# Hybrid scan, retention and latent-attention diffusion step: prologue, early mixer and the stage between scan and attention reordered

## The chip, the cores and the metric

One core of a Trainium2 chip runs the whole program. Time is device microseconds (us) of that core. Engines: TensorE (PE, its weight loads PEld), VectorE (DVE), ScalarE (ACT), GpSimd (POOL), and SyncE (SP), which here only issues DMAs. Every engine works through a list of its own, in order, and waits on semaphores.

## The reference, cut to what matters

128 context tokens and 256 latent tokens (T = 384 columns) run through two layers of width 1024, all in float32:

```python
h = rmsnorm(x) * (1 + scale1) + shift1
u = h @ w_in                      # split among three head groups
y_ssd = rmsnorm((scan_f + scan_b + d_skip * xs) * silu(z)) # xs: conv of width 5, silu
y_ret = silu(g) * groupnorm(retention_f + retention_b)
q = rmsnorm(u_q) @ w_uq           # rank 256, 4 heads, 64 + 32 rotary
k, v = rmsnorm(u_kv) @ w_ukv      # rank 128, cached context keys before
y_mla = softmax(q k / sqrt(96)) v
x = x + gate1 * (concat(y_ssd, y_ret, y_mla) @ w_out)
h = rmsnorm(x) * (1 + scale2) + shift2
x = x + gate2 * swiglu(h)
```

Scales, shifts and gates come from `silu(cond) @ w_ada + b_ada`, 1024 x 6144 a layer.

## The kernel before, in words

Channels lie on the 128 partitions, tokens on the free axis. A float32 product against a big weight is made of three matmuls in a reduced format: weights and activations are each split in a high part (`whi`, `h_hi`) and a rest (`wlo`, `h_lo`); ACT rounds the high part (`split_hi`, L966) and DVE subtracts for the rest (`split_lo`, L1278). Weights come in blocks of 1 MB over two slots of `stage`; SP issues each load when the slot's split is done. `w_in` is 11 blocks of 256 columns (`win_block`), `w_out` 4, the feed-forward 22 and 16. A w_in block leaves PSUM by `win_out` on ACT; in layer 1 DVE first scales it by the norm (`evac`) and ACT adds a shift (`add_shift`). The modulation matmuls (`ada_block`) are strewn between as filler for PE.

**Prologue (layer 0).** SP loads the early constants, the first half of x, weight block 0, the dt weights, block 1, then, after two of ACT's loads have landed, the small weights and the other constants. ACT issues the second half of x and eight chunks of 1 MB of modulation weights (`ada0`, L1014). ACT makes Silu of the condition (for which a table is loaded), loads the table of Exp and Ln again, and squares the second half of x (L1021); DVE squares the first half (L1368) and adds the pairs (L1372); PE sums over partitions (L540). The norm factor is made by `rstd`: ACT's Ln and Exp give a start value, DVE's four steps (L1306 to L1310) refine it. For each of eight chunks PE multiplies (`ada0_chunk`), DVE copies the rows out (`ada0_taken`, L1377), PE sums them (`ada0_sum`, L562), DVE makes scale and shift and h (`modulated`, `normed`, `normed_low`), and PE runs its tiles of dt and block 0 (`dt_tile`, `win_tile`). On DVE the split of block 0 stands after `modulated(0)`.

**Early mixer (both layers).** Blocks 0, 1 and 2 fill the padded `upad`, on which DVE runs a convolution of five taps for three pairs of channel tiles (`conv_pair`, 8 instructions, L1441); ACT makes the first tap (`first_taps`) and the Silu (`silu_channels`, L1037). Step sizes (`step_sizes`) give the decays, whose running sums PE makes (L617 to L629), ACT copies (`cum`, `tedt`, `cd`, `cumt`) and DVE splits (L1499 to L1505). PE then transposes the convolved values of the three chunks (`turn_values`, L640), runs block 4, transposes the keys (L652), and makes the chunk states (L662) from products that POOL computes (L1785) once all copies of the transpositions are there. On DVE the order in layer 1 is: block 0 out, split 2, block 1 out, dt bias, split 3, step sizes, pair 0, block 2 out, the cumulative rows, pair 1 (`conv_pair(2)`), split 4, pair 2, block 3 out. On PE the transposition of the third chunk, which needs block 3 out of PSUM, stands before block 4.

**Scan.** Six steps (chunk, group) follow, each beside one of the blocks 5 to 10.

**Between scan and attention.** PE (L718 to L824): four retention states, two modulation blocks, then for each of three chunks the retention scores, a sum of squares (gated scan output, query latent, key latent, one after the other in PSUM bank 7, `mean_square`), a modulation block, and the retention values; the key rotation; the group mean of the retention output (`mu_ps`), queries (L792) with the group's sum of squares between head 2 and 3, query rotations (L800), keys (L809), values (L817). DVE runs four `rstd` here, three of width T and one of width 2T, and the elementwise work behind each; the buffer `gsq` holds all squares, `rt` the rotated part. Everything must be done, the last `rstd` too, before attention's first score (L847).

## Time and profile before

| | |
|---|---|
| median of 3 runs | 1102.44 us (1101.33 to 1104.98) |
| the profiled execution, its own time | 1104.6 us |
| its span, first to last instruction | 1102.7 us |
| mean granted clock of PE | 0.979 |
| PE busy | 1034.7 us (94%) |
| DVE, ACT, POOL busy | 632.0, 440.1, 98.3 us |
| moved by DMA | 159.56 MB, mean 145 GB/s |

A granted clock of 1.00 is 2.4 GHz, 0.50 is 1.2 GHz. A row of the timeline reads: start, busy us, engine, line, operation, output <- inputs, shape, count, and in brackets the idle time of the engine before it with what ended it. Idle time counts only where it lies on the chain that ends last; a busy time next to idle time of PE says who was waited for. A float32 matmul stands as two records. `q` after an engine marks the DMAs that it issues.

### The profile page before, as it was taken

The numbers are of one execution on the slowest core, as the hardware profiler recorded it, in microseconds if no ns is written. First come the engines' busy times: TensorE is split into PE (matmuls) and PEld (weight loads), VectorE is DVE, ScalarE is ACT, GpSimd is POOL, SyncE is SP. The second block draws the span as 40 slices with busy tenths as digits, with TensorE's granted clock in tenths as the row PEclk, the third lists the DMA queues.
The fourth block names the chain that finished last, engine by engine and source line by source line (L and its number), as shares of the span: only waits on it lengthen the run. The fifth ranks groups of instructions, "written<-read, shape, count | busy, mean of one in ns | idle before, by whom it ended". The sixth has DMA issues, their size and how long they took to land.

```text
span 1102.7 us, 16365 instructions
## 1 busy us (share of the span) xinstructions
PE 1034.7 (94%) x6520; PEld 942.9 (86%) x6520; DVE 632.0 (57%) x1138; ACT 440.1 (40%) x682; POOL 98.3 (9%) x99
## 2 busy tenths in 40 slices
PE   3999997899999999999999599889999999999996
PEld 2697994589999989999999589647899999999995
DVE  5567767657655544434356677685675545544333
ACT  3155446336433332333335444642563334333231
POOL 0003323003000000001000042400010000000010
PEclk9899999899999999999999899998999999999998
DMA  9642345313333468333353222550233333543431
GB/s 386 258 188 86 115 153 190 124 39 122 118 140 123 170 250 313 132 121 129 116 222 153 77 87 79 217 209 1 77 115 114 123 143 115 184 174 105 131 131 57
DMA packets 30679, 159.56 MB, mean 145 GB/s; under 512 B 3425, under 2 KB 4385, under 8 KB 19873
## 3 DMA queue, kind: packets, MB, share of 16 engines
q1 hardware_dynamic: 29328, 149.63, 37.4%
q10 hardware_dynamic: 1296, 9.18, 2.0%
q8 instruction: 38, 0.62, 0.2%
q14 instruction: 17, 0.13, 0.0%
HBM read 156.27 MB, written 2.52 MB: 144 GB/s over the span
## 4 chain that ended last, share of the span: by engine, by line
PE 86%; DVE 8%; ACT 3%; issue 1%; DMA 1%; POOL 0%; DVEq 0%; SPq 0%; ACTq 0%; POOLq 0%
PE ps L464 25%; PE ps L466 24%; PE ps L465 24%; PE ps L491 2%; DVE v L1441 2%; PE ps L865 1%; DVE wlo L1278 1%; PE ps L847 1%; PE ps L792 1%; ACT whi L966 1%; DMA x<-x_dram 1%; PE ps L662 1%; PE ps L856 1%; PE ps L684 1%; PE ps L710 1%
## 5 line engine op out<-in xcount | busy, mean ns | idle before, releaser
L464 PE MATMUL ps<-h_hi,whi 128*128 128x386 f32 (+1 forms) x1120 | 387.7, 346 | 0.2
L466 PE MATMUL ps<-h_hi,wlo 128*128 128x386 f32 (+1 forms) x1120 | 382.4, 341 | 0.0
L465 PE MATMUL ps<-h_lo,whi 128*128 128x386 f32 (+1 forms) x1120 | 381.5, 341 | 0.0
L1278 DVE TENSOR_TENSOR wlo<-stage,whi 128x2048 fp32r<-128x2048 f32 (+1 forms) x106 | 223.4, 2108 | 151.9 <-ACT whi L966 151.9
L966 ACT ACTIVATE whi<-stage 128x2048 fp32r<-128x2048 f32 (+1 forms) x106 | 185.9, 1753 | 228.1 <-PE ps L466 203.9
L464 PEld LDWEIGHTS ps<-h_hi,whi 128*128 128x128 f32 x1120 | 213.5, 191 | 11.1 <-issue 9.7
L465 PEld LDWEIGHTS ps<-h_lo,whi 128*128 128x128 f32 x1120 | 213.9, 191 | 0.3
L466 PEld LDWEIGHTS ps<-h_hi,wlo 128*128 128x128 f32 x1120 | 212.8, 190 | 0.1
L464 PE MATMUL ps<-hid_hi,whi 128*128 128x384 f32 x352 | 118.3, 336 | 0.0
L466 PE MATMUL ps<-hid_hi,wlo 128*128 128x384 f32 x352 | 118.3, 336 | 0.0
L465 PE MATMUL ps<-hid_lo,whi 128*128 128x384 f32 x352 | 118.3, 336 | 0.0
L1326 DVE COPY shifted<-ps 128x4 f32<-128x4 f32 x55 | 8.8, 161 | 109.0 <-PE ps L466 108.6
L466 PEld LDWEIGHTS ps<-hid_hi,wlo 128*128 128x128 f32 x352 | 66.2, 188 | 0.0
L464 PEld LDWEIGHTS ps<-hid_hi,whi 128*128 128x128 f32 x352 | 66.2, 188 | 0.0
L465 PEld LDWEIGHTS ps<-hid_lo,whi 128*128 128x128 f32 x352 | 66.2, 188 | 0.0
L1337 DVE SCALAR_TENSOR_TENSOR x<-ps,modl,x 128x128 f32<-128x128 f32 x96 | 35.4, 410 | 11.6 <-PE ps L466 11.6
L1837 POOL TENSOR_TENSOR ny<-nv 128x384 f32<-128x384 f32 x2 | 2.2, 1093 | 441.5 <-ACT nv L1244 441.5
L491 PE MATMUL ps<-adas,cond 128*32 128x256 f32 x640 | 39.9, 383 | 0.0
L1200 ACT ACTIVATE adas<-ps,att 128x384 f32<-128x384 f32 (+1 forms) x24 | 12.2, 510 | 55.6 <-DVE att L1684 55.6
L491 PEld LDWEIGHTS ps<-adas,cond 128*32 128x32 f32 x640 | 18.1, 109 | 18.2 <-issue 8.7
L1002 ACT ACTIVATE hid_hi<-nt 128x384 f32 (+1 forms) x22 | 11.6, 525 | 51.8 <-DVE nt L1726 51.8
L1002 ACT ACTIVATE hid_hi<-ny 128x384 f32 (+1 forms) x22 | 11.6, 525 | 51.7 <-DVE ny L1726 51.7
(269 smaller groups left out, 1147.2 us busy)
## 6 DMA issues: line engine op xcount, KB each, us to landing
stage<-wf_dram SPq DMA_DIRECT2D x44, 1024.0 KB, 4.8
adas<-wada_dram SPq DMA_DIRECT2D x80, 512.0 KB, 5.6
stage<-win_dram SPq DMA_DIRECT2D x22, 1024.0 KB, 4.8
stage<-wf_dram SPq DMA_DIRECT2D x32, 704.0 KB, 4.1
stage<-wout_dram SPq DMA_DIRECT2D x8, 1024.0 KB, 5.4
adaf<-wada_dram ACTq DMA_DIRECT2D x6, 1024.0 KB, 17.6
small<-small_dram SPq DMA_DIRECT2D x2, 1202.5 KB, 9.0
adas<-wada_dram ACTq DMA_DIRECT2D x2, 1024.0 KB, 29.9
```

The lines of the kernel that those rows point to most:

```text
L464: mm(out, ah, bh, start=(k == 0), stop=False)
L465: mm(out, ah, bl, start=False, stop=False)
L466: return mm(out, al, bh, start=False, stop=(k == n - 1))
L491: last = mm(ps[j * CW:(j + 1) * CW, 4, half * 256:half * 256 + 256], cond[:, k, :], adas[:, b % 4, j * 256:(j + 1) * 256], start=(b == 0), ...
L662: last = mm(ps[d * 64:d * 64 + 64, 6 - s // 2 * 2, g * 256:g * 256 + 256], bt[:, c, g * 64:g * 64 + 64], vte[s][:, g * 256:g * 256 + 256], ...
L684: last = mm(ps[:, 5 + d, hh * P:hh * P + P], sel[:, h:h + 1].to_broadcast([P, P]), cumt[:, i0:i0 + P], start=True, stop=True)
L966: f(whi[:, g % 2, 0:width], stage[:, g % 2, 0:width], ACT.Copy).then_inc(w_hi, 1)
L1002: f(hid_hi[:, bass.ds(i * 2 + j, 1), :], (ny, nt)[j][:, 1:2, :], ACT.Copy).then_inc(hid_hi_ready, 1)
L1200: f(pr[:, i % 2, 0:nk * P], ps[:, i % 2, 0:nk * P], ACT.Exp, bias=att[:, 1, i:i + 1], scale=SCALE, accum_out=att[:, 2, i:i + 1]).then_inc( ...
L1278: tt(wlo[:, g % 2, 0:width], stage[:, g % 2, 0:width], whi[:, g % 2, 0:width].bitcast(F32), ALU.subtract)\
L1337: last = stt(xm, ps[:, bank:bank + 1, t0:t1], gm, xm, ALU.mult, ALU.add)
L1441: ins = stt(v[:, a, :], upad[:, a, w:w + CONVT], sc(C_CW + w * 6 + a), v[:, a, :], ALU.mult, ALU.add)
```

## The change

No arithmetic is added or left out except that two of the norms share one `rstd`, so that a layer has five. What is moved:

- Prologue: the first half of x is loaded by ACT's queue, ahead of the second; SP holds weight block 1 back until chunk 1 of `ada0` has landed. ACT squares its half of x before the Silu of the condition (the table of Exp and Ln is loaded ahead of it, Silu's and again Exp's behind it), and splits block 0 before `rstd`. DVE splits block 0 first of all; the row copy of chunk 1 comes after `modulated(0)`.
- Early mixer: on DVE pair 0 comes before block 1 in layer 1, pair 1 right after the step sizes in both layers. On ACT the cumulative rows come before `win_out(2)` and its split; the first taps of pair 2 come after the first four Silus; the copy of the third transposition comes after the stacked copies. On PE `turn_values(2, 0)` stands after block 4. POOL waits chunk by chunk.
- Scan to attention: the squares of both latents go to the upper half of `h_hi` (`sq_b`) right after block 10 and are summed, in banks 0 and 1, ahead of everything; one `rstd` of width 2T serves both. Queries come before the last two retention states, rotations between scores and values of the retention. The gated squares go to `h_lo` (`sq_c`). The group's `rstd` is moved behind the values and is waited for only by attention's first output; on DVE it still stands before `ada_rows` and the first maximum. `rt` lies in `late`.

Cut to its core:

```diff
-RSTD = 6
+RSTD = 5
+        with ExitStack() as place:
+            sq_b, sq_c = (sb(n, [P, KD, TB], F32, place)[:, KW2:KD, 0:T] for n in ("sq_b", "sq_c"))
```

SP:

```diff
-            sp.dma_start(x[:, 0:KD // 2, :], x_d[:, 0:KD // 2, :]).then_inc(x_in0, 16)
                 load_dt(L)
+                if L == 0:
+                    sp.wait_ge(ada0_in[1], 16)
                 load_win(L, 1)
```

PE, early mixer:

```diff
                 turn_values(0, 6)
                 turn_values(1, 7)
+                win_block(L, 4)
                 pe.wait_ge(u_raw if L else u_ready, 4)
                 turn_values(2, 0)
-                win_block(L, 4)
```

PE, scan to attention:

```diff
+                pe.wait_ge(gsq_ready, L * 4 + 2)
+                pe.wait_ge(u_raw if L else u_ready, 10)
+                for m in range(3):
+                    last = mm(ps[:, m // 2, 0:T], ones, sq_b[:, m, :], start=(m != 1), stop=(m != 0))
+                last.then_inc(ms_ready, 1)
+                ret_states((0, 1))
+                pe.wait_ge(ssd_y, L * 3 + 3)
+                ada_block(L * 6 + 3, 0, 2)
+                ada_block(L * 6 + 3, 1, 2)
                 pe.wait_ge(qn_ready, L * 2 + 2)
...
                     last.then_inc(q_ps, 1)
+                ret_states((2, 3))
+                pe.wait_ge(u_ready, L * N_WIN + N_WIN)
+                ret_scores(0)
+                mm(ps[hrow, 7, 0:LAT], perm, u[hrow, U_KR, CTX:T], start=True, stop=True).then_inc(krot_ps, 1)
+                ada_block(L * 6 + 3, 2, 2)
...
+                ret_values(0)
+                ret_scores(1)
+                pe.wait_ge(gsq_ready, L * 4 + 3)
+                pe.wait_ge(kr_ready, L * 3 + 3)
+                for m in range(4):
+                    last = mm(ps[:, 7, 0:T], ones, sq_c[:, m, :], start=(m == 0), stop=(m == 3))
+                last.then_inc(ms_ready, 1)
+                ret_values(1)
+                ret_scores(2)
+                ada_block(L * 6 + 3, 3, 2)
+                ret_values(2)
+                ada_block(L * 6 + 3, 4, 2)
...
+                ada_block(L * 6 + 3, 5, 2)
+                pe.wait_ge(q_ready, L * 2 + 2)
+                pe.wait_ge(centred, L + 1)
+                pe.wait_ge(gsq_ready, L * 4 + 4)
+                for m in range(2):
+                    last = mm(ps[:, 5 + m, 0:T], cc(K_BD), ry2[:, m, :], start=True, stop=True)
+                last.then_inc(ms_ready, 1)
+                ada_block(L * 6 + 3, 6, 2)
                 ada_block(L * 6 + 3, 7, 2)
-                pe.wait_ge(rstd_ready, L * RSTD + 6)
+                        if a == 0:
+                            pe.wait_ge(rstd_ready, L * RSTD + 5)
```

ACT:

```diff
+            act.dma_start(x[:, 0:KD // 2, :], x_d[:, 0:KD // 2, :]).then_inc(x_in0, 16)
             act.dma_start(x[:, KD // 2:KD, :], x_d[:, KD // 2:KD, :]).then_inc(x_in1, 16)
...
+            use_exp_and_ln()
+            act.wait_ge(x_in1, 16)
+            for k in range(KD // 2, KD):
+                f(sq[:, k, :], x[:, k, :], ACT.Square).then_inc(sq0_ready, 1)
             act.wait_ge(const_in, 16)
             act.wait_ge(zeroed, 2)
...
             use_exp_and_ln()
+            split_hi(0, 0)
             rstd(1, ps[:, 7:8, 0:T], 1, 1.0 / D)
-            split_hi(0, 0)
                 first_taps(2)
-                win_out(2)
-                split_next(2)
...
-                first_taps(4)
+                win_out(2)
+                split_next(2)
                 for t in range(4):
                     silu_channels(t)
+                first_taps(4)
                         if q == 5:
+                            act.wait_ge(w_used, L * NB + N_WIN + 2)
+                            f(sq_b[:, 0:2, :], u[:, U_MQ:U_MQ + 2, :], ACT.Square).then_inc(gsq_ready, 1)
+                            f(sq_b[:, 2, :], u[:, U_CKV, :], ACT.Square).then_inc(gsq_ready, 1)
...
+                            f(ny[:, 0, :], ps[:, 0, 0:T], ACT.Ln, bias=eps, scale=1.0 / RANKQ)
+                            f(ny[:, 1, :], ps[:, 1, 0:T], ACT.Ln, bias=eps, scale=1.0 / RANKKV).then_inc(ln_ready, 1)
+                            act.wait_ge(ln_ready, L * RSTD + 2)
+                            f(ny[:], ny[:], ACT.Exp, scale=-0.5).then_inc(y0_ready, 1)
```

DVE:

```diff
+            split_lo(0, 0)
             ada0_taken(0)
             rstd(1, ps[:, 7:8, 0:T], 1, 1.0 / D)
             normed(0)
-            ada0_taken(1)
             for m in range(KD):
                 modulated(m)
                 if m == 0:
-                    split_lo(0, 0)
+                    ada0_taken(1)
                     split_dt(0)
                     split_lo(L, 2)
+                    conv_pair(0)
...
                     step_sizes()
-                    conv_pair(0)
+                conv_pair(2)
+                if L:
                     evac(2)
...
-                conv_pair(2)
                 split_lo(L, 4)
```

DVE, scan to attention, the new order: the latents' `rstd`, query scale, `ret_end(0)`, `ret_end(1)`, key latent's scale, gated product, `ret_end(2)`, `ret_end(3)`, `ret_probs(0)`, key rotation and `kh`, two query rotations, `ret_probs(1)`, `split_lo`, the gated `rstd`, `ret_probs(2)`, gated scale, `ry`, four `mix_low`, `centred`, `mixer_gates`, the group's `rstd`, `ada_rows`.

POOL:

```diff
-                pool.wait_ge(tr_ready, L * 4 + 4)
                 for s, (c, d) in enumerate(STATE_JOBS):
+                    pool.wait_ge(tr_ready, L * 4 + c + 1)
```

## Rows read from the trace of the kernel before

**Rows 1.** The page's chain that ended last: shares of the span by engine

```profile
PE 86%; DVE 8%; ACT 3%; issue 1%; DMA 1%; POOL 0%; DVEq 0%; SPq 0%; ACTq 0%; POOLq 0%
```

**Rows 2.** Busy us (count) of PE, PEld, DVE, ACT, POOL by stretch; then clock, DMA

```profile
26.88:58.50 31.62, 29.30 (x201) 22.08 (x201) 16.92 (x46) 5.75 (x9) 0.00 (x0) 0.85 0.67 263
58.50:99.52 41.02, 38.89 (x310) 35.05 (x310) 31.09 (x58) 25.54 (x40) 1.79 (x3) 1.00 0.42 154
166.62:210.43 43.81, 35.52 (x292) 19.44 (x288) 33.99 (x57) 24.07 (x38) 7.84 (x11) 1.00 0.55 197
585.64:634.31 48.67, 36.91 (x289) 33.54 (x289) 32.10 (x65) 24.00 (x42) 1.79 (x3) 0.89 0.35 130
607.70:619.13 11.43, 1.12 (x9) 0.85 (x8) 11.22 (x20) 1.17 (x3) 0.00 (x0) 0.73 0.27 93
639.00:699.00 60.00, 60.00 (x404) 57.30 (x402) 47.88 (x107) 30.64 (x59) 20.00 (x18) 1.00 0.34 124
701.86:746.25 44.39, 35.53 (x292) 19.44 (x288) 34.13 (x57) 24.62 (x40) 7.70 (x11) 1.00 0.52 195
```

**Rows 3.** Prologue: DMA issues (KB, us to landing), then timeline rows

```profile
x<-x_dram SPq DMA_DIRECT2D x1, 768.0 KB, 8.4
stage<-win_dram SPq DMA_DIRECT2D x1, 1024.0 KB, 9.2
...
7.07 1.28 ACT L1010 ACT_TABLE_LOAD   x1
8.36 1.76 ACT L1021 ACTIVATE sq<-x 128x384 f32<-128x384 f32 x4
...
12.33 4.45 PE L540 MATMUL ps<-sq,const 128*128 128x384 f32 x8 [12.33 <-DVE sq L1372]
```

**Rows 4.** Prologue, timeline: start, us, engine, line, what, idle before

```profile
...
18.19 0.55 DVE L1306 TENSOR_SCALAR nv<-ps 128x384 f32<-128x384 f32 x1
...
20.42 0.56 DVE L1380 TENSOR_TENSOR sq<-x,nv 128x384 f32<-128x384 f32 x1
...
22.20 2.29 DVE L1278 TENSOR_TENSOR wlo<-stage,whi 128x2048 fp32r<-128x2048 f32 x1
...
26.88 0.48 PE L464 MATMUL ps<-h_hi,dthi 128*16 128x384 f32 x1
```

**Rows 5.** Mixer of layer 1, timeline

```profile
585.81 0.16 DVE L1326 COPY shifted<-ps 128x4 f32<-128x4 f32 x1 [4.28 <-PE ps L466]
...
593.95 4.73 DVE L1441 SCALAR_TENSOR_TENSOR v<-upad,small,v 128x388 f32<-128x388 f32 x8
...
610.80 1.15 ACT L1037 ACTIVATE v<-v,small 128x388 f32<-128x388 f32 x2 [3.38 <-DVE v L1441]
...
612.00 1.11 PE L640 MATMUL ps<-const,v 128*128 128x128 f32 x8 [4.29 <-ACT v L1037]
...
619.13 1.12 PE L640 MATMUL ps<-const,v 128*128 128x128 f32 x4 [6.02 <-DVE u L1433]
...
634.31 1.99 PE L662 MATMUL ps<-ew,bt 128*64 128x256 f32 x8 [1.29 <-POOL ew L1785]
```

**Rows 6.** Mixer of layer 0, timeline of PE

```profile
85.03 1.53 PE L640 MATMUL ps<-const,v 128*128 128x128 f32 x12 [0.56 <-ACT v L1037]
...
99.52 1.99 PE L662 MATMUL ps<-ew,bt 128*64 128x256 f32 x8 [1.29 <-POOL ew L1785]
```

**Rows 7.** Between scan and attention: two groups of layer 0, then timeline

```profile
L792 PE MATMUL ps<-u,small 128*96 128x384 f32 x16 | 5.6, 491 | 0.0
L722 PE MATMUL ps<-gsq,const 128*128 128x384 f32 x14 | 5.3, 508 | 3.0 <-DVE nv L1310 3.0
...
199.42 0.96 DVE L1306 TENSOR_SCALAR nv<-ps 128x768 f32<-128x768 f32 x1 [1.62 <-ACT ny L978]
...
203.26 0.69 DVE L1665 TENSOR_TENSOR rt<-ps,const 32x512 f32<-32x512 f32 x1
...
709.37 0.71 PE L745 MATMUL ps<-u 64*128 64x128 f32 x8 [2.73 <-DVE small L1602]
```

More of the change, by code:

```diff
@@ L312, in program @@
             lat = slice(LATC + 2, LATC + 2 + LAT)
+            rt = late.rearrange("p (a t) -> p a t", a=2)
             rmt = [upad[:, 2 * d:2 * d + 2, lat].rearrange("p o (m i) -> p o m i", m=2) for d in range(2)]
@@ L809, in _ @@
                     mm(ps[:, 2 + hp, 0:512], small[:, c0:c0 + 128], ck[:, 0:512], start=True, stop=True).then_inc(k_ps, 1)
+                pe.wait_ge(ry_taken, L + 1)
+                for m in range(2):
+                    last = mm(ps[:, m, 0:T], cc(K_BD), ry[:, m, :], start=True, stop=True)
+                last.then_inc(mu_ps, 1)
                 wv = small[:, C_UKV + 256:C_UKV + 512]
-                pe.wait_ge(rstd_ready, L * RSTD + 5)
+                pe.wait_ge(rstd_ready, L * RSTD + 4)
                 for kt in range(4):
@@ L1018, in _ @@
             use_exp_and_ln()
-            act.wait_ge(x_in1, 16)
-            for k in range(KD // 2, KD):
-                f(sq[:, k, :], x[:, k, :], ACT.Square).then_inc(sq0_ready, 1)
+            split_hi(0, 0)
             rstd(1, ps[:, 7:8, 0:T], 1, 1.0 / D)
-            split_hi(0, 0)
             split_dt(0)
@@ L1169, in _ @@
                 f(kr[rrow, CTX:2 * P], small[rrow, C_KR:C_KR + P], ACT.Copy).then_inc(kr_ready, 1)
+                for h in range(HM):
+                    act.wait_ge(q_ps, L * HM + h + 1)
+                    f(qh[0:96, h, :], ps[0:96, h % 2, 0:T], ACT.Copy).then_inc(q_taken, 1)
+                act.wait_ge(ssd_gated, L * 2 + 2)
+                f(sq_c, u[:, U_Z:U_Z + 4, :], ACT.Square).then_inc(gsq_ready, 1)
                 split_hi(L, N_WIN + 1)
-                rstd(L * RSTD + 2, ps[:, 7:8, 0:T], 1, 1.0 / (HS * 64))
-                f(gsq[:, 0:2, :], u[:, U_MQ:U_MQ + 2, :], ACT.Square).then_inc(gsq_ready, 1)
-                f(gsq[:, 2, :], u[:, U_CKV, :], ACT.Square).then_inc(gsq_ready, 1)
+                rstd(L * RSTD + 3, ps[:, 7:8, 0:T], 1, 1.0 / (HS * 64))
                 act.wait_ge(w_used, L * NB + N_WIN + 2)
@@ L1177, in _ @@
                     mix_high(L, k, u[:, U_Z + k, :])
-                rstd(L * RSTD + 3, ps[:, 7:8, 0:T], 1, 1.0 / RANKQ)
-                rstd(L * RSTD + 4, ps[:, 7:8, 0:T], 1, 1.0 / RANKKV)
-                for h in range(HM):
-                    act.wait_ge(q_ps, L * HM + h + 1)
-                    f(qh[0:96, h, :], ps[0:96, 2 + h % 2, 0:T], ACT.Copy).then_inc(q_taken, 1)
-                    if h == 0:
-                        act.wait_ge(centred, L + 1)
-                        f(ry2[:], ry[:], ACT.Square).then_inc(gsq_ready, 1)
-                    if h == 1:
-                        rstd(L * RSTD + 5, ps[:, 0:2, 0:T], 2, 1.0)
                 for h in range(HM):
@@ L1193, in _ @@
                     f(vm[:, kt, :], ps[:, 2 if kt % 2 else 7, 0:256], ACT.Copy).then_inc(vm_ready, 1)
+                act.wait_ge(centred, L + 1)
+                f(ry2[:], ry[:], ACT.Square).then_inc(gsq_ready, 1)
+                rstd(L * RSTD + 4, ps[:, 5:7, 0:T], 2, 1.0)
                 for i in range(NATT + 2):
@@ L1667, in _ @@
                     tt(q, q, rt[rrow], ALU.add).then_inc(q_ready, 1)
+                ret_probs(1)
+                split_lo(L, N_WIN + 1)
+                dve.wait_ge(qn_ready, L * 2 + 2)
+                dve.wait_ge(ck_ready, L * 3 + 3)
+                rstd(L * RSTD + 3, ps[:, 7:8, 0:T], 1, 1.0 / (HS * 64))
+                ret_probs(2)
+                for m in range(4):
+                    z = u[:, U_Z + m, :]
+                    stt(z, z, sc(C_SN + m), nv[:, 0, :], ALU.mult, ALU.mult).then_inc(mix_src, 1)
+                dve.wait_ge(ry_ps, L * 3 + 3)
+                nc.vector.tensor_copy(ry[:], ps[:, 0:2, 0:T]).then_inc(ry_taken, 1)
+                for m in range(4):
+                    mix_low(L, m, u[:, U_Z + m, :])
+                dve.wait_ge(mu_ps, L + 1)
+                dve.wait_ge(ry_taken, L + 1)
+                tt(ry[:], ry[:], ps[:, 0:2, 0:T], ALU.subtract).then_inc(centred, 1)
+                mixer_gates(L)
+                dve.wait_ge(mix_src, L * 6 + 4)
+                rstd(L * RSTD + 4, ps[:, 5:7, 0:T], 2, 1.0)
                 ada_rows(L * 6 + 3, 2)
@@ L1714, in _ @@
                 split_lo(L, FFN + 1)
-                rstd(L * RSTD + 6, ps[:, 7:8, 0:T], 1, 1.0 / D)
+                rstd(L * RSTD + 5, ps[:, 7:8, 0:T], 1, 1.0 / D)
                 def ffn_tile(i, j, width):
```

118 lines of the change are left out of this document (42 added, 76 removed).

## The prediction

> **What bounds the kernel now.** I read the chain of work that ended last first: TensorE (PE) holds 86% of it and the vector engine (DVE) 8% [rows 1]. So time can be won only where PE stands idle or runs at the lower of its clocks, and a reordering is worth what it takes out of those places. The table by stretch says where they are [rows 2]: from 26.88 to 58.50 PE is busy 29.30 of 31.62 us but at a mean granted clock of 0.85; in the mixer of layer 0 it idles 41.02 - 38.89 = 2.1 us; in the same place of layer 1 48.67 - 36.91 = 11.8 us, with a clock of 0.89; between scan and attention 43.81 - 35.52 = 8.3 and 44.39 - 35.53 = 8.9 us. The scan of layer 1 (639 to 699) is busy 60.00 of 60.00: what is won before such a stretch is kept to its end, nothing in it absorbs or adds. Then I followed, instruction by instruction, what each idle stretch waits for.
>
> **Prologue.** Now: the first half of x rides the SP queue and lands 8.4 us after issue; the squares of the other half run on ACT at 8.36 for 1.76 us, behind a table load at 7.07 (1.28 us); PE starts at 12.33 and takes 4.45 us [rows 3]. DVE runs the first rstd from 18.19 to 20.42, modulates, and then splits weight block 0 (2.29 us from 22.20) before it does what PE's first tile needs; that tile starts at 26.88 [rows 4]. The change puts x on the ACT queue ahead of everything, so both halves should land by about 7; DVE's four products and the pair sums follow the ACT squares (1.76 us from 7.2 to 9.0). The price is a Silu table load and a load back, 2 x 1.28 us, now between the squares and the split: the condition vector, for which PE's first matmul waits, is ready at 9.0 + 1.28 + 0.2 = 10.5 instead of 7.1. PE starts at 10.5, not 12.33, and ends its squares between 14.2 and 15.6, by when the clock rises. But DVE now has the split of block 0 ahead of everything. Block 0 is issued at 5.85 and landed 9.2 us later [rows 3], behind x on its queue; without x ahead of it I estimate 13.0 (the 1 MB took 5.45 us once x had landed at 9.6; the flow now starts at about 7.5). ACT splits to 14.9, DVE 2.2 us to 17.1, then row copy and rstd (2.23 us) to 19.7, modulation to 21.3, and the row copy of chunk 1, two normalising products and a tile to 23.9: PE's tile at about 24.8. That is **-2.1 us**. Bounds: if block 0 lands at 15.05 as now, the chain ends where it ended (0); if at 11.5, the squares bind and it is -3.5. From there the loop of eight steps is unchanged, one transfer behind the other landing before it is wanted. The clock was low for nearly half of it; a shift of one rise or fall is worth up to 2 us either way.
>
> In these rows a table load costs its 1.28 us and the next ACT instruction follows at once (7.07 + 1.28 = 8.35, square at 8.36 [rows 3]). The Trainium skill (ScalarE: Activation LUTs, What ACT_TABLE_LOAD costs) has every switch cost about 1.38 us of drain more, 2.66 us in all, which speaks against the new order, since two switches lie ahead of PE's first matmul. By it PE would start at 13.3, the prologue would be worth -0.7 and the whole sum -12.7. I take the row.
>
> **Mixer, layer 1.** Now: the first convolution pair stands behind the step sizes (DVE 593.95, 4.73 us) though DVE idled 4.28 us before 585.81 with its taps ready; the second pair comes after the cumulative rows at 606.6, so ACT's Silu of it starts at 610.80 after 3.38 us of waiting, PE transposes at 612.00 (idle 4.29), and the third transposition waits for u at 619.13 (idle 6.02), with weight block 4 queued behind it and PE at half clock by then [rows 5]. The change: the first pair fits into the idle stretch, 581.8 to 586.5, which makes block 1's evacuation 0.7 us late; nobody waits for that before 598. Bias, split and step sizes end at 594.1 as now, the second pair runs to 598.8, the evacuation of block 2 to 599.8. ACT copies the cumulative rows at 599.1, adds the shifts (1.5), splits (1.9), loads the table (1.28) and does four Silus (2.3): 606.9. PE ends block 3 at 607.5 and goes on without a wait: two transpositions, block 4 (8.7) and the third to 617.8, four modulation blocks (1.86) to 619.6, the keys' transposition to 620.2. What is late next is ACT: the taps of the third pair only at 608.0 (DVE idles 2 us before it), that pair 4.7, block 3's evacuation to 613.7, shifts, split, two copies, two Silus, table, the four stacked copies, the third copy and the one PE needs: 1.5 + 1.9 + 1.1 + 1.1 + 1.3 + 1.7 + 0.5 + 0.5 = 9.6, so 623.4. PE idles 3.2 us there. POOL, which now waits chunk by chunk, has three of four products done by then. The state matmuls start at 623.5 where they stood at 634.31 [rows 5]: **-10.8 us**. Bounds: with a new fall of the clock -8; with no late ACT at all, PE's own work only, -13.
>
> **Mixer, layer 0.** The same moves: the wait of 0.56 us at 85.03 goes, since the second pair runs in DVE's idle time before the cumulative rows, and the one of 1.29 us for POOL before 99.52 [rows 6], since POOL and ACT's copies are done before PE gets there. By the same stepping the state matmuls start at 97.3: **-2.2 us**, bounds -1.3 and -2.5. The two queues moved past (the output copy of block 2 and the split after it, behind the cumulative rows on ACT) are needed by nobody before block 4.
>
> **Scan to attention.** PE's work stays (35.5 us [rows 2]): three squares matmuls in one go for both latent norms and four for the gated one, as seven now (14 half records of 508 ns [rows 7]). One of four narrow rstd chains goes, as the two latent ones become one wide one (0.96 us a step [rows 7]). So count PE's idle time from the end of the scan's last product (166.62). The squares are ready then; matmuls 2.1, two Ln and an Exp 2.0, DVE products 0.9 + 3 x 1.0, query scale 1.2: ready at 175.1, and PE has only states (1.0) and two modulation blocks (1.9) beside it: idle 3.4. Queries (5.6 us for four heads [rows 7]) and the held-back states run to 181.7. From 181.3 DVE is the bound: two state sums, retention weights, the key rotation and its copy (about 4.3 together), two query rotations of 2.1 (203.26 to 205.37 [rows 7]), weights, the split 2.2, an rstd 2.2, weights: 195.4. PE idles about 0.3 before it and 2.5 in it. Then retention values, keys, means, values: waits of 0.2 at the copies, 0.4 for ACT's square of the centred values (queued behind four copies), 0.2 to 1 for the last modulation block, whose buffers come free late. The last rstd, wide, (3.84 us from 199.42 now [rows 7]) moves to the very end, ahead of the row copy and the first maximum of attention: that maximum waits till 211.2, 2.1 after PE's last score. Idle: 3.4 + 0.3 + 2.5 + 0.2 + 0.4 + 0.2 + 2.1 = 9.1 against 8.3: **+0.8 us** in layer 0, **+0.2** in layer 1, whose stage is 0.6 longer now and comes out the same. DVE's chain has simply another wait put in place of each one taken away. Bounds for each, nearest rows: -3 (no idle before the queries at all) and +4 (the low clock).
>
> **Sum.** -2.1 - 2.2 - 10.8 + 0.8 + 0.2 = -14.1 us. The profiled execution took 1104.6 us for a span of 1102.7, so it would take 1090.5; the median shown is 2.2 lower, which gives 1088.3. About 0.3% (3.3 us) is what a measurement of this kernel tells from no change.
>
> **Rivals.** (1) The clock falls in the new idle time. PE idles 3.4 us where it idled 2.73 before 709.37 with the clock held [rows 7]; between 607.70 and 619.13, with waits of 4.29 and 6.02 us, it fell to half (mean 0.73) [rows 2, 5]. The new gap lies between. Five to seven us of work at 1.2 GHz instead of 2.4 cost some 3.4 a layer: 1095. The Trainium skill (TensorE: Matmul & The Clock Gate, HAM oscillation) says that idle gaps between bursts throttle the array again; by that this rival would be the likely one. Chance 0.2. (2) The stage does better than I stepped: its DVE queue is full from 181 on and I may have mis-placed a wait; with the 2.5 us before the last retention values and the 0.8 gone in each layer, and a prologue of -3.5: 1080 to 1083. Chance 0.12. (3) The mixer's change doesn't do what it says: if the taps or the evacuation of block 2 come late, the third transposition still waits, half of 10.8 is left, and the table loads eat the prologue's gain: 1096. Chance 0.06. (4) Slower: one whole stage between scan and attention, whose matmul bursts are now thinner, stays at 1.2 GHz end to end; 35.5 us of work take 71, less the 8.9 of idle that absorb it, +27: 1115. It decides from about 14 us lost to the low clock in both stages together. Against it: the mean clock in both is 1.00 now [rows 2]. Chance 0.03.
>
> Forecast case 0.59; the thin tails of rivals 1 and 3 end within 0.3%. Range 1080.5 to 1096.5: cases 2 and 3 nearly whole, most of 1. Faster 0.92, same 0.04, slower 0.04.
>
> **What would show it.** PE without idle time between block 3 and the third transposition in layer 1, DVE's third pair there waiting about 2 us for ACT; PE's first matmul near 10.5 and first tile near 24.8; an idle stretch of some 3.4 us before the queries; the first maximum waiting for the wide rstd. Wrong would be: a mixer gain in layer 1 under 7 us, block 0 landing no earlier than 15, or a stage that shrinks by over 3 us a layer.

## The result, and the profile after

| | before | after |
|---|---|---|
| median | 1102.8 us (5 runs) | 1097.28 us (1095.55 to 1098.3, 5 runs) |
| ratio | | 0.9947, 95% interval 0.9932 to 0.9961 |
| profiled execution, own time | 1104.6 us | 1096.78 us |
| its span, mean granted clock | 1102.7 us, 0.979 | 1094.9 us, 0.974 |

The kernel is 5.5 us faster. Forecast were 14 us, and 1097.28 lies just above the upper end of the range, 1096.5. The trace and the runs below say where the rest went. By stretch, the answer to [rows 2] (stretch, its length, busy us and count of PE, PEld, DVE, ACT, POOL, then the clock, DMA share, GB/s):

```profile
28.06:59.00 30.94, 28.61 (x209) 21.88 (x210) 17.30 (x49) 7.18 (x11) 0.00 (x0) 0.94 0.64 254
59.00:96.25 37.25, 37.08 (x302) 34.03 (x301) 31.20 (x54) 22.95 (x38) 7.74 (x5) 1.00 0.46 170
161.45:209.61 48.16, 37.60 (x290) 20.27 (x288) 34.21 (x53) 23.45 (x36) 8.95 (x12) 0.93 0.45 161
690.00:738.21 48.21, 37.63 (x288) 20.13 (x287) 34.12 (x54) 24.02 (x38) 8.88 (x12) 0.93 0.44 161
169.89:177.90 8.01, 8.01 (x16) 3.64 (x16) 3.19 (x6) 2.84 (x7) 0.00 (x0) 0.66 0.29 115
```

The mixer's idle time is gone in layer 0. The stage between scan and attention is 4.4 us longer in layer 0 (48.16 against 43.81) and 4.0 in layer 1 (first maximum 738.21, against 746.25; the scan ends 12.1 us earlier, at 689.8, the maximum comes only 8.0 earlier). DVE's and ACT's work there is what it was. PE's is 2.1 us more although it has the same matmuls, since its clock was 0.93 and not 1.00; its idle time is 10.6 us and not 8.3.

**Prologue**, the answer to [rows 3, 4], timeline:

```profile
9.32 1.28 ACT L1038 ACT_TABLE_LOAD   x1
10.93 4.81 PE L545 MATMUL ps<-sq,const 128*128 128x384 f32 x8 [10.93 <-ACT cond L1038]
15.13 1.91 ACT L982 ACTIVATE whi<-stage 128x2048 fp32r<-128x2048 f32 x1 [3.00 <-DMA stage<-win_dram]
17.07 2.29 DVE L1298 TENSOR_TENSOR wlo<-stage,whi 128x2048 fp32r<-128x2048 f32 x1 [6.93 <-ACT whi L982]
19.76 0.61 PE L567 MATMUL ps<-const,adac 128*128 128x2 f32 x4 [3.02 <-DVE adac L1397]
23.77 1.01 PE L567 MATMUL ps<-const,adac 128*128 128x2 f32 x4 [2.40 <-DVE adac L1397]
28.06 0.48 PE L469 MATMUL ps<-h_hi,dthi 128*16 128x384 f32 x1
```

PE starts at 10.93 (10.5 forecast), and the table loads cost 1.28 us each with the next instruction right behind (the Silu at 10.62), as in the row of before. But block 0, issued at 5.88, lands at 15.1, as it did with 768 KB of x ahead of it on its queue. Everything on DVE now stands behind its split: the row copies of chunks 0 and 1 come late, PE waits 3.02 and 2.40 us for them, and the first tile is at 28.06, not 24.8; before it was at 26.88. From the end of DVE's split to that tile it is 8.7 us (7.7 forecast): behind the second of these waits PE ran at half clock, and the third chunk's sixteen matmuls took 1.93 us, where the first two chunks' took 1.07 each.

A single execution says little here. In the profiles of all runs the first tile comes at 27.96 to 28.35 us with the changed prologue and at 26.88 to 28.47 with the old one, and the mean clock from 28 to 60 us is either 0.85 to 0.87 or 0.91 to 0.96, whichever prologue the kernel has.

**Mixer.** First PE in layer 0 beside the same rows of before, then layer 1, the answer to [rows 5, 6]. Layer 0 after, timeline:

```profile
96.25 1.09 PE L667 MATMUL ps<-ew,bt 128*64 128x256 f32 x8
97.17 1.08 PE L667 MATMUL ps<-amat,bt 128*64 128x256 f32 x8
```

Layer 0 before, timeline (its first row is in [rows 6]):

```profile
101.43 2.08 PE L662 MATMUL ps<-amat,bt 128*64 128x256 f32 x8
```

Layer 1 after, timeline:

```profile
581.13 4.73 DVE L1461 SCALAR_TENSOR_TENSOR v<-upad,small,v 128x388 f32<-128x388 f32 x8 [0.26 <-ACT v L1092]
604.08 2.15 ACT L1055 ACTIVATE v<-v,small 128x388 f32<-128x388 f32 x4
607.28 4.73 DVE L1461 SCALAR_TENSOR_TENSOR v<-upad,small,v 128x388 f32<-128x388 f32 x8 [2.19 <-ACT v L1092]
622.12 0.41 PE L504 MATMUL ps<-const,adac 128*128 128x128 f32 x2 [2.89 <-DVE adac L1308]
622.46 1.96 PE L667 MATMUL ps<-ew,bt 128*64 128x256 f32 x8
```

The state matmuls start 3.3 us earlier in layer 0. Between the first tile and them PE idles 2.0 us less, 2.5 us more come from the higher clock in the stretch up to 59.00 (0.94 and not 0.85), and the later first tile takes 1.2 back; only the 2.0 are the new order's own. In layer 1 they start 11.85 us earlier (layer 1 itself began 0.7 us earlier). PE has no idle time between block 3 and the third transposition any more, and waits 2.89 us later on (3.2 forecast). The state matmuls are themselves shorter: in layer 0 the sixteen records took 3.99 us before (from 99.52 to the end of the row at 101.43), with the same clock of 1.00, and take 2.00 us now: before, each pair had to wait for POOL's next product, and POOL now starts chunk by chunk. That gain I had not counted.

**Between scan and attention, layer 0**, the answer to [rows 7], timeline:

```profile
169.89 8.10 PE L781 MATMUL ps<-u,small 128*96 128x384 f32 x16 [3.47 <-DVE u L1646]
177.92 0.97 PE L731 MATMUL ps<-stm,xt 128*64 128x64 f32 x16
178.64 0.41 DVE L1623 TENSOR_TENSOR late_r<-late_r,ps 64x256 f32<-64x256 f32 x1 [5.50 <-PE ps L731]
179.06 2.84 POOL L1851 TENSOR_TENSOR ew<-u,upad 64x256 f32<-64x256 f32 x4 [13.46 <-PE ps L731]
182.22 1.54 DVE L1671 COPY kh<-kr 32x2048 f32<-32x2048 f32 x1
185.00 1.01 DVE L1679 TENSOR_TENSOR qh<-qh,late 32x512 f32<-32x512 f32 x1
193.93 0.44 PE L753 MATMUL ps<-ew,xt 128*64 128x128 f32 x4 [2.30 <-DVE ew L1631]
205.16 0.96 DVE L1326 TENSOR_SCALAR nv<-ps 128x768 f32<-128x768 f32 x1 [4.86 <-ACT ny L994]
209.61 0.28 DVE L1713 TENSOR_REDUCE att<-ps 128x1 f32<-128x128 f32 x1
```

PE idles 3.47 us before the queries (3.4 forecast). The granted clock is 0.66 over the queries (the last window above), so most of them run at half (1.2 GHz), and they take 8.10 us and not 5.6 [rows 7]. Only behind them does PE make the last two states, for which DVE has waited 5.50 us by then, and for which POOL waits as well. So POOL's query products, which before ran at 169.7 and were over at 176.7, now run beside DVE's rotations. The copy of the rotated key takes 1.54 us (1.22 before), the sum that ends the first rotation 1.01 (0.68 before).

### The profile page after: what moved, and what is told of

Same layout as the page of the kernel before. It is cut to its first block, busy times and chain, and to the rows that moved or that the text cites. A ratio compares the mean times of both kernels' runs of the same rounds, so it can differ in the third digit from the quotient of the medians.

```text
span 1094.9 us, 16355 instructions
## 1 busy us (share of the span) xinstructions
PE 1035.5 (95%) x6520; PEld 943.2 (86%) x6520; DVE 634.8 (58%) x1132; ACT 441.9 (40%) x681; POOL 107.1 (10%) x99
## 4 chain that ended last, share of the span: by engine, by line
PE 87%; DVE 8%; ACT 2%; DMA 1%; issue 1%; DVEq 0%; ACTq 0%
PE ps L469 25%; PE ps L471 24%; PE ps L470 24%; PE ps L496 2%; PE ps L881 1%; PE ps L781 1%; DVE wlo L1298 1%; DVE v L1461 1%; PE ps L861 1%; DMA stage<-win_dram 1%; ACT whi L982 1%; PE ps L714 1%; PE ps L870 1%; PE ps L689 1%; PE ps L556 1%
## 5 line engine op out<-in xcount | busy, mean ns | idle before, releaser
L469 PEld LDWEIGHTS ps<-h_hi,whi 128*128 128x128 f32 x1120 | 212.6, 190 | 10.7 <-issue 8.8
```

The lines of the kernel that those rows point to most:

```text
L469: mm(out, ah, bh, start=(k == 0), stop=False)
```

## The experiments

Each ran beside the kernel before on the same chip, in three groups: the median of before was 1102.65 us beside runs 1 to 4, 1102.23 beside runs 5 to 8 and 1103.0 beside runs 9 to 12. Differences of about 1 us are read only within a group. The changed kernel itself (1097.28) belongs to none of them, so what is compared with it carries about 1 us of doubt.

**Run 1, the stage undone.** The changed kernel with all hunks of the stage between scan and attention taken back:

```diff
-RSTD = 5
+RSTD = 6
...
-                ret_states((0, 1))
...
+                for s, (c, d) in enumerate(STATE_JOBS):
...
```

> The changed kernel with the stage between scan and attention as it was before (prologue and mixer changed). Theory 1 (that stage costs 4.4 us in layer 0 and 4.0 in layer 1 of what the other two parts win): the stage takes 43.8 and 44.4 us again from the scan's last product to the first maximum, and the kernel 1089 us against 1102.8 before and 1097.3 changed. Theory 2 (a later end of the scan or other traffic is what lengthens the stage, not its own order): the stage stays near 48 us and the kernel near 1097.

Measured: 1088.39 us (4 runs), ratio 0.9865 (0.9850 to 0.9880). The stage is 44.3 and 44.9 us long (the windows shown begin 0.1 and 0.2 us behind its start). Windows:

```profile
162.15:206.35 44.20, 37.12 (x290) 20.12 (x287) 34.16 (x57) 24.02 (x38) 7.75 (x11) 0.96 0.55 196
686.73:731.44 44.71, 37.05 (x288) 19.87 (x286) 34.30 (x56) 24.50 (x39) 7.56 (x11) 0.96 0.52 193
```

So it is the stage's own order that costs 8.9 us (1097.28 - 1088.39), as theory 1 has it. In the profiles 7.4 of them lie within the stage (48.2 and 48.4 us against 44.3 and 44.9); the rest was not placed. Even the old order now has some low clock in it (0.96): where the clock falls is not fixed by the order of the stage alone.

**Run 2, the stage alone.** Only those hunks, on the kernel before.

```diff
-RSTD = 6
+RSTD = 5
...
+                ret_states((0, 1))
...
```

> Only the stage between scan and attention changed, prologue and mixer as before. Theory 1: slower by 8.4 us, 1111 us; idle of 3.5 us before the queries in both layers, and a fall of the granted clock to half behind it. Theory 2 (the longer stage comes from its earlier start): no slower than 1104.

Measured: 1110.41 us (5 runs), ratio 1.0066 (1.0052 to 1.0079): 7.8 us slower. PE idles 3.48 us before the queries of both layers. Behind it the queries take 7.09 us in layer 0 and 5.40 in layer 1: the fall of the clock that theory 1 expected in both came in one. By itself this part of the change is a loss.

**Run 3, the mixer alone.** Only the mixer's hunks, on the kernel before.

```diff
+                    conv_pair(0)
                     dve.wait_ge(dt_taken, L + 1)
                     evac(1)
...
-                    conv_pair(0)
+                conv_pair(2)
+                if L:
                     evac(2)
...
```

> Only the early mixer changed. Theory 1 (the mixer is worth 2.3 us in layer 0 and 11.1 in layer 1, and nothing behind it gives that back): 1089.5 us. Rival (part of what the mixer wins comes from the prologue's shift of the clock, or is given back in the scan): 1093 or more. The difference to the run with prologue and mixer is the prologue's worth: 0.9 us by theory 1, 2.1 as predicted.

Measured: 1087.10 us (4 runs, 1086.05 to 1089.32), ratio 0.9859 (0.9841 to 0.9877): 15.5 us faster, 2.1 more than theory 1's 13.4 and nothing given back. With run 1 (1088.39) the prologue's worth is +1.3 us, a loss, too small to be told from nothing. The 15.5 us may hold some chance too: the profile before had the low clock up to 60 us (0.87 from 28 to 60), this run's had 0.95.

**Run 4, block 0 early.** Run 1 with:

```diff
+            dve.sem_inc(w_split, 2)
             nc.vector.memset(cond[:], 0.0).then_inc(zeroed, 1)
...
             dve.sem_inc(rstd_ready, 1)
-            dve.sem_inc(w_split, 2)
```

> Prologue and mixer changed, stage as before, and weight block 0 released to SP at the start (DVE's increment of the release stands ahead of its wait for the constants), so that it is issued near 1 us instead of 5.88. Theory 1 (block 0's landing at 15.05 is what holds the first tile at 28.06): it lands by 10, the split is over before the squares are summed, first tile 2 to 3.5 us earlier, kernel 2 to 3 us under the run without it. Rival (x lands later by what block 0 takes, and the squares come later by as much, or the clock takes it back): first matmul after 11.5, kernel within 1 us of the run without it.

Measured: 1088.14 us (4 runs), 0.25 under run 1: no difference. The timeline:

```profile
10.29 1.77 ACT L1020 ACTIVATE sq<-x 128x384 f32<-128x384 f32 x4 [2.52 <-DMA x<-x_dram]
13.69 5.46 PE L541 MATMUL ps<-sq,const 128*128 128x384 f32 x8 [13.69 <-ACT cond L1023]
14.90 1.91 ACT L967 ACTIVATE whi<-stage 128x2048 fp32r<-128x2048 f32 x1
27.96 0.48 PE L465 MATMUL ps<-h_hi,dthi 128*16 128x384 f32 x1
```

Block 0 is issued at 1.20 us and lands 8.9 us later, by 10.1. ACT's split no longer waits for it, but the second half of x is there only at 10.29 (7.80 in run 1), and PE starts at 13.69 (11.19 in run 1). The rival is right: the second half of x comes later, and with it everything that starts from the squares. The first tile is at 27.96, against 28.35 in run 1.

**Run 5, the states first.** The changed kernel with:

```diff
                 ada_block(L * 6 + 3, 1, 2)
+                ret_states((2, 3))
+                pe.wait_ge(u_ready, L * N_WIN + N_WIN)
+                ret_scores(0)
+                mm(ps[hrow, 7, 0:LAT], perm, u[hrow, U_KR, CTX:T], start=True, stop=True).then_inc(krot_ps, 1)
                 pe.wait_ge(qn_ready, L * 2 + 2)
...
-                ret_states((2, 3))
-                pe.wait_ge(u_ready, L * N_WIN + N_WIN)
-                ret_scores(0)
...
+                ret_end(0)
+                ret_end(1)
                 n, y, t = nv[:], ny[:], nt[:]
```

> The changed kernel with the last two retention states, the first retention scores and the key rotation moved ahead of the queries on PE, and the copy of the first two states ahead of the latent rstd on DVE. Theory 1 (the stage is long because PE has nothing before the queries, lets the clock fall there, and DVE then stands 5.5 us for states that PE makes only behind the queries): 2.4 us of the 3.5 us of idle time are filled, the clock holds, DVE's 5.5 us of waiting go; POOL's query products move beside the latent rstd and cost it up to 1.3 us. 3 to 4 us less a layer: 1090 to 1091. Rival (DVE has too much to do in this stage whatever the order; contention with POOL sets the time): the queries come 1.3 us later, idle time moves behind them, within 2 us of 1097.3.

Measured: 1089.86 us (4 runs), ratio 0.9887 (0.9871 to 0.9903): 7.4 us under the changed kernel. Timeline:

```profile
167.27 4.24 POOL L1850 TENSOR_TENSOR ew<-u,upad 64x256 f32<-64x256 f32 x4 [1.89 <-PE ps L731]
171.06 7.09 PE L785 MATMUL ps<-u,small 128*96 128x384 f32 x16 [2.72 <-DVE u L1647]
172.42 2.70 DVE L1656 TENSOR_TENSOR u<-u,v 128x512 f32<-128x512 f32 x2
175.05 0.40 DVE L1623 TENSOR_TENSOR late_r<-late_r,ps 64x256 f32<-64x256 f32 x1
```

DVE no longer waits for the states (175.05, no idle time). POOL's products now run beside the latent rstd and the gating (2.70 us for what took 1.82), and the queries come later for it. PE idles 2.72 us there, and over the queries the clock falls in layer 0 but not in layer 1, where they take 5.40 us after 2.71 us of idle time. The stage is 44.6 and 45.0 us long, 3.6 and 3.4 less than in the changed kernel.

**Run 6, filler.** The changed kernel with:

```diff
                 ada_block(L * 6 + 3, 1, 2)
+                pe.wait_ge(u_ready, L * N_WIN + N_WIN)
+                for m in range(4):
+                    mm(ps[:, 3, 0:T], ones, sq_b[:, m % 3, :], start=True, stop=True)
```

> The changed kernel with four matmuls of no use (their output is overwritten) in PE's idle time before the queries. Nothing starts earlier; only the clock can change. Theory 1 (the fall of the clock costs 2.5 us in layer 0 and 1.2 in layer 1 in the queries, besides what follows from it): queries 5.6 us at full clock in both layers, 1093.5. Rival (the time is the idle stretch's own and the late work behind is bound by DVE, which waits for its states no matter what): same within 1 us, 1097.

Measured: 1092.44 us (5 runs), ratio 0.9904 (0.9891 to 0.9918): 4.8 us under the changed kernel, by nothing but useless work. Timeline:

```profile
165.97 2.85 PE L776 MATMUL ps<-sq_b,const 128*128 128x384 f32 x8
169.52 5.40 PE L784 MATMUL ps<-u,small 128*96 128x384 f32 x16 [0.70 <-DVE u L1649]
175.56 0.41 DVE L1626 TENSOR_TENSOR late_r<-late_r,ps 64x256 f32<-64x256 f32 x1 [2.80 <-PE ps L731]
```

The queries run at the full clock (2.4 GHz), and DVE's wait for the states falls from 5.50 to 2.80 us. So with the order as it is, 4.8 of the 8.9 us that the stage costs are the clock and what stands behind the slow queries. They fall unevenly: the stage is 3.0 us shorter in layer 1, where the clock is 1.00 throughout, and only 1.1 in layer 0, where it fell later, behind the 2.30 us wait for DVE (the next sixteen modulation matmuls take 1.94 us and not 1.07).

**Run 7, POOL held.** The changed kernel with:

```diff
                 pool.wait_ge(rst_ps, L * 4 + 4)
+                pool.wait_ge(q_ready, L * 2 + 2)
```

> The changed kernel with POOL's eight retention query products held back until DVE has rotated the queries. Theory 1 (DVE's small operations are slowed by POOL working beside them): the copy of the rotated key falls from 1.54 to 1.22 us, the last product of the first rotation from 1.01 to 0.68, DVE reaches the end of the rotations 1.2 us earlier; but PE then waits for POOL before the second retention values, 2 to 3 us, so the kernel is slower by about 1 to 3 us a layer: 1099 to 1103. Rival (these durations come from the operands or from PE's or ACT's accesses, not from POOL): the durations stay.

Measured: 1098.22 us (7 runs, 1097.31 to 1101.66), 0.9 above the changed kernel, which is not clear of noise and a little less than expected. Timeline:

```profile
169.79 5.40 PE L781 MATMUL ps<-u,small 128*96 128x384 f32 x16 [3.47 <-DVE u L1646]
178.81 1.22 DVE L1671 COPY kh<-kr 32x2048 f32<-32x2048 f32 x1
181.27 0.68 DVE L1679 TENSOR_TENSOR qh<-qh,late 32x512 f32<-32x512 f32 x1
189.50 0.69 PE L753 MATMUL ps<-ew,xt 128*64 128x128 f32 x4 [5.26 <-POOL ew L1852]
```

Its clock over the queries, windows:

```profile
169.79:175.10 5.31, 5.31 (x16) 2.53 (x16) 3.19 (x6) 2.84 (x7) 0.00 (x0) 1.00 0.38 152
```

The durations fall exactly as theory 1 says, to 1.22 and 0.68 us. From the first sum of states to the end of the rotations DVE takes 8.2 us (175.84 to 184.06), where run 6, also at the full clock, takes 9.5 (175.56 to 185.04): contention costs 1.3 us, and 1.3 in layer 1 by the same rows. The run shows one thing more: the same 3.47 us of idle time, and in layer 0 the queries at the full clock. There the clock fell later, behind the 5.26 us wait for POOL (0.50 from 189.50 to 193.00). In layer 1 the same idle time was followed by queries of 8.25 us. Idle time goes ahead of each of these falls and doesn't say where they come.

**Run 8, run 5 without the prologue.** Run 5 with the prologue's hunks taken back:

```diff
-            act.dma_start(x[:, 0:KD // 2, :], x_d[:, 0:KD // 2, :]).then_inc(x_in0, 16)
...
-            split_lo(0, 0)
             ada0_taken(0)
...
```

> Mixer as changed, prologue as before, stage as changed but with the order of the run with the states first. If the prologue is worth nothing or costs about 1 us, and the states first win 7 us: 1089 to 1090, just above the run with the mixer alone (1087.1). Rival (the prologue helps where the stage is as changed): 1092 or more.

Measured: 1091.27 us (4 runs), 1.4 above run 5. So here the changed prologue wins 1.4 us, where between runs 3 and 1 it lost 1.3. The number lies between my two expectations. The profiles differ most in a place that has nothing to do with the prologue: behind the same idle time of 2.71 us the queries of layer 1 take 8.38 us here and 5.40 in run 5.

**Run 9, run 5 with filler.** Three of the useless matmuls ahead of the last two states.

```diff
                 ada_block(L * 6 + 3, 1, 2)
+                pe.wait_ge(u_ready, L * N_WIN + N_WIN)
+                for m in range(3):
+                    mm(ps[:, 3, 0:T], ones, sq_b[:, m % 3, :], start=True, stop=True)
                 ret_states((2, 3))
```

> The run with the states first, with three matmuls of no use in the 2.7 us that PE still idles before the queries. There the queries took 7.09 us in layer 0 and 5.40 in layer 1. Theory 1 (the idle time in front of the queries decides whether they run at the low clock): 5.4 us in both, 1.7 us less: 1088.2. Rival (where the clock falls is a matter of where the stretch happens to lie, and idle time of this length alone does not decide it): the fall moves to another place and the time stays within 0.5 us of 1089.9.

Measured: 1087.68 us (4 runs, 1087.53 to 1090.11), ratio 0.9867 (0.9852 to 0.9882), 2.2 under run 5, with the reserve that they stand in different groups. The queries take 5.40 us in both layers, as theory 1 has it, but that is not where the time was won. In layer 0 the low clock came later instead (0.94 from 176.00 to the first maximum, 1.00 from 178.20 in run 5), so that the stage is 44.5 us long and not 44.6, and in layer 1 it is 44.5 and not 45.0. Most of the rest lies behind layer 1's first maximum (355.5 us to the end of the span, 356.8 in run 5), where the kernels are the same. The rival has the mechanism and missed the time.

**Run 10, more moves.** Run 9 with:

```diff
                 ada_block(L * 6 + 3, 3, 2)
+                ada_block(L * 6 + 3, 4, 2)
                 ret_values(2)
-                ada_block(L * 6 + 3, 4, 2)
...
+                ret_probs(2)
                 rstd(L * RSTD + 3, ps[:, 7:8, 0:T], 1, 1.0 / (HS * 64))
-                ret_probs(2)
...
```

and the copy of the retention output, its centring and ACT's square moved forward as the expectation says.

> The run before this one, with these moves: the last retention weights on DVE ahead of the gated rstd, the copy of the retention output and its centring ahead of the products beside them, ACT's square of the centred values after two of the four value copies, and modulation block 4 on PE ahead of the last retention values. If the stage's second half is bound by DVE's order (PE idle 2.30 us before the last values, DVE 4.86 us before the wide rstd), PE's 2.3 us go and the wide rstd starts 2 to 3 us earlier: 2 us less a layer, 1084. Rival (DVE's amount of work binds, not its order): within 1 us of the run before this one.

Measured: 1086.33 us (5 runs, 1084.7 to 1086.59), ratio 0.9841 (0.9828 to 0.9854), 1.3 us under run 9. That is a third of what I expected. Timeline:

```profile
193.21 0.70 PE L827 MATMUL ps<-small,ck 128*128 128x256 f32 x2 [1.41 <-ACT kh L1209]
194.85 1.51 PE L827 MATMUL ps<-small,ck 128*128 128x256 f32 x4 [0.94 <-ACT vm L1212]
201.13 0.96 DVE L1329 TENSOR_SCALAR nv<-ps 128x768 f32<-128x768 f32 x1 [6.81 <-ACT ny L996]
203.67 0.64 PE L496 MATMUL ps<-adas,cond 128*32 128x256 f32 x8 [2.17 <-DMA adas<-wada_dram]
```

The 2.3 us before the last values are gone, but PE now waits for ACT's copies (1.41, 0.94) and for the last modulation block's transfer (2.17); DVE is done earlier and waits 6.81 us instead of 4.86 for ACT's start value. The bound had moved to ACT and to that transfer. The stage is 44.2 us long in layer 0, 0.3 less than in run 9, and 42.6 in layer 1, 1.9 less.

**Run 11, run 10 without the prologue.** The same hunks taken back as in run 8.

```diff
-            act.dma_start(x[:, 0:KD // 2, :], x_d[:, 0:KD // 2, :]).then_inc(x_in0, 16)
...
```

> The same as the run before this one with the prologue of before. Without the stage's change the changed prologue cost 1.3 us, with it it won 1.4. Theory 1 (it is worth nothing, and what differs is where the clock falls): within 1.5 us of the run before this one, to either side. Rival (the changed prologue wins 1 to 2 us here too): slower by 1.5 or more.

Measured: 1085.67 us (5 runs, 1085.46 to 1088.36), 0.7 below run 10. Three pairs now: +1.3, -1.4, +0.7. The changed prologue is worth nothing that can be told from zero.

**Run 12, the last rstd spread out.** Run 10 with:

```diff
-                rstd(L * RSTD + 4, ps[:, 5:7, 0:T], 2, 1.0)
+                dve.wait_ge(ln_ready, L * RSTD + 4)
+                ts(nv[:], ps[:, 5:7, 0:T], -0.5, -0.5 * EPS, ALU.mult, ALU.add).then_inc(wide_ps, 1)
                 ada_rows(L * 6 + 3, 2)
                 for i in range(NATT + 1):
+                    if i == 4:
+                        dve.wait_ge(y0_ready, L * RSTD + 4)
+                        step(tt(nt[:], ny[:], ny[:], ALU.mult))
...
```

The other two steps stand at i = 5 and 6, what used them at 7 to 11, and attention's first output waits for the two readers of the sums in PSUM.

> The run with the moves (no. 10), with three of the four steps of the last, wide rstd taken out of DVE's path before the first maximum and put between the fifth, sixth and seventh maxima of attention. The first maximum waited for 3.84 us of it plus the row copy. If the start of attention waits for DVE there: 2 us less a layer than no. 10, 1080. Rival (attention's first steps are bound by DVE's own chain, or the last modulation blocks' transfers hold PE instead): less than 1 us in all.

Measured: 1080.72 us (5 runs, 1078.14 to 1082.95), ratio 0.9792 (0.9774 to 0.9809). It is 5.6 us under run 10, 16.6 under the changed kernel and the fastest of all. The number came as expected (1080), but not where it was expected. Windows, run 10 first:

```profile
161.48:205.58 44.10, 38.35 (x294) 20.79 (x294) 34.90 (x53) 23.04 (x35) 8.51 (x12) 0.96 0.49 177
685.85:728.37 42.52, 36.98 (x294) 20.24 (x294) 34.90 (x53) 23.79 (x39) 8.66 (x12) 0.99 0.50 179
```

Run 12:

```profile
163.67:206.98 43.31, 38.36 (x295) 20.71 (x294) 32.13 (x51) 23.05 (x35) 8.53 (x12) 0.96 0.49 172
685.12:726.97 41.85, 37.01 (x295) 20.25 (x294) 32.12 (x50) 23.79 (x39) 8.66 (x12) 1.00 0.49 174
```

The stage loses 0.8 and 0.7 us, of 2 expected each. The rest came out right behind the first maximum: from it to the fifth it is 10.7 us in run 10 and 8.7 in run 12, and in layer 1 10.4 and 8.2. The longer stretches agree: from the first maximum of layer 0 to that of layer 1 it is 522.8 us in run 10 (205.58 to 728.37) and 520.0 in run 12, 0.7 of it the stage's, and from there to the end of the span 356.4 and 354.0. That is 6.0 us in all. The two profiles differ by only 3.8, since in run 12's the stage of layer 0 began 2.2 us later: up to there the programs are the same, the first tile is at 28.14 and 28.15, and the clock from 28 to 60 was 0.94 in one and 0.85 in the other. That much a single execution moves by itself. In the changed kernel and in run 10 DVE has two products with the rstd's result (0.61 and 0.56 us) ahead of the second and the third maximum; now they come behind the seventh and eighth, where DVE has idle time between the maxima. Before the fifth it still waits for PE. Timeline of run 12:

```profile
215.71 0.56 DVE L1727 TENSOR_REDUCE att<-ps 128x1 f32<-128x384 f32 x1 [4.08 <-PE ps L864]
```

## Why the prediction was wrong, point by point

**Prologue, -2.1 forecast, 0 measured** (three pairs, +1.3, -1.4, +0.7). The step that failed is "without x ahead of it I estimate 13.0". Block 0 lands 9.2 us after issue with or without x ahead of it on its queue: the rest of x and the modulation chunks are loaded at the same time by ACT's queue, in both kernels, and the new order only moves 768 KB from one queue to the other (and holds block 1 back). Run 4 shows the same from the other side: issued 4.9 us earlier, block 0 takes 8.9 us, and x comes 2.5 us later. The bound I had set for a landing at 15.05, a worth of 0, is what came. The Trainium skill (DMA: Bandwidth & Descriptors, Queues, rings and completion order) has each DMA engine go round-robin over the queues that have work; the row agrees with it in so far as a load does not wait for its own queue alone. Why 768 KB less ahead of it on its queue gave nothing at all, no run shows. PE's start was right within 0.4 us; it was not what decides, since DVE's split stood ahead of the row copies. One reading was off besides: a mean clock of 0.85 from 26.88 to 58.50 is the low clock for about 30% of it, not "nearly half"; that went into no term.

**Mixer, -13.0 forecast, -15.5 measured** (run 3). The place of each wait was right: DVE's third pair in layer 1 waits 2.19 us for ACT's taps (2 forecast), and DVE has block 3 out of PSUM by 613.0 (613.7 forecast). The state matmuls come 11.85 us earlier, 11.2 of them within layer 1 (10.8 forecast). The term missing is POOL's pace during those matmuls, some 2 us in layer 0: I had counted POOL's change only as the wait in front of them. How much of the 2.5 us between forecast and run is the clock before 60 us, no run separates.

**Scan to attention, +1.0 forecast, +8.9 measured** (run 1 against the changed kernel; +7.8 in run 2). This step failed most. The idle times that I named were stepped nearly right (3.47 before the queries, 2.30 before the last values), and wrong was what follows from them. First, the clock: rival 1, with a chance of 0.2 and 3.4 us a layer, came true. Filling the idle time wins 4.8 us in all (run 6). The row I leaned on, 2.73 us of idle time with the clock held [rows 7], was no evidence for a threshold: run 5 had a fall and none at 2.7 us, run 7 none and a fall at 3.47. Second, "queries and the held-back states run to 181.7. From 181.3 DVE is the bound" hid a wait on the path: DVE has nothing to do from 173 on until PE, behind four queries, makes two states of 1 us. Run 5 puts them ahead of the queries and wins 7.4 us. The first and the second cause overlap and are not to be added: with the filler in both, the states first still win 4.8 us (run 9 against run 6, of different groups), while with the states first the filler takes only 0.6 us more out of the two stages. At the full clock DVE waits 2.80 us for the states, at the low one 5.50, so what the clock costs goes mostly through that wait, and the order is the larger part. Third, the move of a PE job moved POOL's job, which waits for it, beside DVE's rotations; that costs 1.3 us a layer (run 7) and no step of mine followed POOL. The net loss is smaller, since before POOL slowed the gating instead (2.27 us, now 1.82). The Trainium skill (SBUF — State Buffer, Who interferes with whom) has a vector instruction with two operands in SBUF contend with a GpSimd instruction that reads SBUF, and one with at most one operand in SBUF, outside certain faster modes, not. Most rows agree: the weights product, whose other operand is in PSUM, took 0.69 us beside POOL as alone, the sum of two SBUF tiles 1.01 and not 0.68. But the product with the cosines just ahead of that sum, two SBUF tiles too, took 0.67 in both runs; it began at 184.29, and the POOL instruction beside it at 184.33. So two operands in SBUF are not enough to be slowed.

**Sum.** The three parts err by +2.1, -2.5 and +7.9 us, 7.5 of the 9.0 between forecast and median. 0.4 is the median of before, 1102.8 in this comparison for the 1102.44 that I started from. The last 1.1 is what the parts, measured one by one in other groups, do not add up to. Of the rivals, 1 was the right one and too low in chance; DVE's wait for the states is in none of them. Neither it nor the range held the kernel, since it adds to the two errors besides it, and I had let each rival stand alone.

## What to carry to other kernels

When work is moved on one engine, step every engine that waits for it, and ask of each wait that a short job ends whether that job could stand ahead of the long one. An idle stretch of PE of about 3 us costs its own length and perhaps the clock behind it; cover it with real work. A few matmuls of no use are a cheap test of what the clock takes, if one then looks where the low clock has gone. Before a change is made to explain a difference of 2 us, look whether two executions of one program differ by as much. A chain of elementwise steps needed only later can be spread over a stretch in which another engine is the bound; here that was worth 5.6 us, where the reordering of run 10 was worth 1.3.

## What the runs showed of the hardware that I had not expected

- Useless matmuls made the kernel 4.8 us faster (run 6).
- The same idle time, 3.47 us, was followed by queries of 8.10 and 6.78 us in the two layers of the changed kernel and of 5.40 and 8.25 in run 7; 2.7 us by 7.09 and 5.40 within one run (run 5).
- Up to the stage between scan and attention runs 10 and 12 are the same program, and their profiles are 2.2 us apart there: the clock from 28 to 60 us was 0.94 in one and 0.85 in the other.
- POOL slows only some of DVE's instructions: 0.68 to 1.01 us for a sum of two SBUF tiles, 1.22 to 1.54 for a copy; unchanged are 0.67 for a product of two SBUF tiles that began just ahead of POOL's, and 0.69 for a product with a PSUM operand.
- A 1 MB load took 9.2 us from issue to landing whether 768 KB stood ahead of it on its queue or not.
